# Six more weight blocks of a two-layer model as seven block products, with two of the four weight sums on GpSimd

## The chip, the cores and the metric

The kernel runs on one core of a Trainium2 chip. The metric is the time of one execution on the device in microseconds (us), the median of several runs. The engines are TensorE (PE; its weight loads are PEld), VectorE (DVE), ScalarE (ACT), GpSimd (Pool) and SyncE (SP, which issues most transfers). Each takes its instructions in the order written, and waits on semaphores that others raise.

## The reference

Two layers on 256 tokens of width 1024, all float32. Each layer is a mixer, a layer norm, a mixture of 16 experts (two per token) and a layer norm.

```python
def _mixer_ab(x, ...):                 # layer 0
    proj = x @ w_in                    # 1024 x 6152
    ...                                # retention (4 heads) and mLSTM (4 heads, causal conv on q and k)
    return concat([y_ret, y_ml]) @ w_out

def _mixer_cd(x, ...):                 # layer 1
    proj = x @ w_in                    # 1024 x 6176
    gq, gk, gv, gr, ga, sz, sxbc, sdt = split(proj)
    log_alpha = log_sigmoid(ga @ gla_w_alpha + gla_b_alpha) / 16
    y_gla = head_norm(gla(gq, gk, gv, log_alpha)) * silu(gr)      # 4 heads
    xs, bm, cm = split(silu(causal_conv(sxbc)))
    y = ssd(xs * dt, dt * a, bm, cm) + d * xs                     # 4 groups of 4 heads
    y_ssd = head_norm(y * silu(sz))
    return concat([y_gla, y_ssd]) @ w_out
```

## The kernel before, in words

**Units.** The input weights of a mixer are cut into twelve units of 1024 rows by 512 columns (2 MB), ab0 to ab11 and cd0 to cd11, each in a slot of a ring of six. Both halves of a slot are loaded by SP as soon as the unit six places ahead has been used up. In layer 1, cd0 and cd1 are the queries and keys of the linear attention (GLA), cd2 and cd3 its values, cd4 and cd5 its gate, cd6 to cd9 the inputs of the causal convolution, cd10 and cd11 the gate z of the state-space part (SSD). A *token unit* leaves tokens on the partitions (16 matmuls of 512 columns), a *feature unit* leaves features there (32 of 256 columns). Every float32 matmul shows as two records in the trace.

**A unit as seven products.** ab2 to ab11 are computed otherwise (`first_product`, `other_products`, line 833 for the token form and 836 for the feature form). Tokens and weights are cut into 2 by 2 blocks, and seven products of 4 matmuls of 256 columns (or 8 of 128) give what eight blocks would. Some factors are sums of blocks: two token sums at first and two more (`mix_tokens`), and four weight sums per unit. In the order in which TensorE makes them, the products are:

1. first: bank 0 or 3, plain blocks; ScalarE copies it (`first_copy`)
2. second: bank 1, plain blocks; VectorE adds it (`blend` 0)
3. third: onto the first, with weight sum `sums[0]`; ScalarE copies (`sum_copy` 0)
4. fourth: bank 2 afresh, with weight sum `sums[1]`
5. fifth: onto the third, with the weight block that was changed in place; ScalarE copies (`sum_copy` 1), VectorE adds bank 2 (`blend` 1)
6. sixth: onto the fifth; ScalarE copies (`sum_copy` 2)
7. seventh: onto bank 2, with the block that is changed in place last; VectorE adds (`blend` 2)

The first product of the next unit is made between the fifth and the sixth, in `gap`; `fill` is work of another kind between the second and the third. The semaphore `product_done` counts the second, third, fifth, sixth and seventh product, `combined` the blends, `copied` the later copies. A unit's fourth product waits until all blends of the unit before are done, and its seventh until its own second blend is.

All four weight sums are made by VectorE (`mix_weights`: three; `mix_last`: the fourth, after the second product). They are 128 partitions by 1024 elements each.

**The second mixer's side work.** Each engine's order is written out by hand. VectorE: copies of cd0 and cd1, the gates' running sums (`alpha`, four scans into `bcum`), then per head `gla_head` (scaled queries and eight blocks of scaled keys, whose exponentials ScalarE makes), `p_gla` (masked scores), `y_gla` (norm and gate; it waits for a root from ScalarE). TensorE makes `s_gla` (scores) once `gla_head` is done and `y_gla` (values) once `p_gla` is. Then `taps` (the conv's three later taps per tile on VectorE, the first and the SiLU on ScalarE), `ssd_args`, `ssd_probs`, `ssd_gate`, `ssd_norm` per group, between `s_ssd` and `y_ssd` on TensorE. GpSimd only issues some transfers: among them the store of the SSD running sums and their reload, spread over all partitions, in two halves.

## Time and profile before

| | |
|---|---|
| median of 3 runs | 972.47 us (971.17 to 973.62) |
| the profiled execution | 973.6 us, span 971.8 us |
| TensorE busy | 939.7 us, 97% |
| VectorE busy | 358.6 us, 37% |
| ScalarE busy | 233.4 us, 24% |
| GpSimd busy | 15.3 us, 2% |
| HBM read | 277.04 MB |

The span is from the first instruction to the last in the trace; the execution's own time is measured around it. Busy time of TensorE is from the start of matmuls to their modelled ends, so two neighbouring groups overlap a little: the time from start to start is the better price. The first mixer runs to about 250 us, its experts to 476, the second mixer from there to about 737, its experts to the end.

### The profile page before, as it was taken

What the parts mean: (1) busy time and instruction counts of PE and PEld (TensorE: products, weight loads), DVE (VectorE), ACT (ScalarE), POOL (GpSimd) and SP (SyncE); (2) the same over time, 40 slices, a digit from 0 to 9 for tenths busy, and PEclk for the clock granted to TensorE, in tenths of its full rate; (3) what the DMA queues carried; (4) which work ended last, traced back from release to release, by engine and by line L of the source; (5) the groups of instructions that cost most, each with busy time, mean ns of one, the idle gap of its engine ahead of it and who ended that gap; (6) DMA issues with size and microseconds to landing.
All of it is one profiled execution on the core that took longest, in us unless ns stands there. A gap on an engine that the chain in (4) does not pass through costs nothing.

```text
span 971.8 us, 10789 instructions
## 1 busy us (share of the span) xinstructions
PE 939.7 (97%) x4272; PEld 550.7 (57%) x4272; DVE 358.6 (37%) x847; ACT 233.4 (24%) x497; POOL 15.3 (2%) x29
## 2 busy tenths in 40 slices
PE   8999999999999999999999999999999999999996
PEld 7888988844533454332584568887545334443332
DVE  4656687423522111120335334654225121131204
ACT  1123352420311121110303343432522121111101
POOL 2000000000000000000000000000000000000001
PEclk9999999999999999999999999999999999999999
DMA  8974434462999999999995234434646999999994
GB/s 273 341 263 170 154 111 169 146 244 98 349 379 421 422 416 423 398 419 417 392 326 213 87 104 156 173 131 170 221 173 259 351 421 421 420 422 419 419 419 169
DMA packets 66934, 278.87 MB, mean 287 GB/s; under 512 B 8980, under 2 KB 9344, under 8 KB 44096
## 3 DMA queue, kind: packets, MB, share of 16 engines
q1 hardware_dynamic: 65008, 271.60, 71.9%
q0 software_dynamic: 1872, 6.53, 1.7%
q8 instruction: 37, 0.61, 0.3%
q14 instruction: 17, 0.14, 0.0%
HBM read 277.04 MB, written 1.06 MB: 286 GB/s over the span
## 4 chain that ended last, share of the span: by engine, by line
PE 83%; DMA 10%; DVE 3%; issue 1%; ACT 1%; SPq 0%; DVEq 0%
PE bank L766 67%; PE bank L833 10%; DMA ring<-in_moe_w_up 7%; DMA ring<-in_moe_w_down 2%; PE bank L1212 2%; PE bank L836 2%; DMA ring<-in_w_in_ab 1%; PE bank L1217 1%; PE bank L1607 1%; PE bank L925 1%; DVE feat L2333 1%; ACT feat L1675 0%; PE bank L1119 0%; PE bank L1160 0%; DVE stat L2642 0%
## 5 line engine op out<-in xcount | busy, mean ns | idle before, releaser
L766 PE MATMUL bank<-ring,feat 128*64 128x512 f32 (+1 forms) x1152 | 228.7, 595 | 3.0 <-ACT feat L1675 2.7
L766 PE MATMUL bank<-ring,hT 128*64 128x512 f32 (+1 forms) x544 | 159.3, 595 | 7.2 <-DMA ring<-in_moe_w_up 3.6
L766 PEld LDWEIGHTS bank<-ring,feat 128*64 128x64 f32 (+1 forms) x1152 | 74.2, 131 | 142.6 <-issue 131.0
L1675 ACT ACTIVATE feat<-bank 32x512 f32<-32x512 f32 (+3 forms) x128 | 60.9, 494 | 382.1 <-PE bank L766 241.4
L766 PE MATMUL bank<-hT,ring 128*128 128x256 f32 x640 | 140.2, 380 | 0.8 <-DMA ring<-in_w_in_ab 0.8
L766 PEld LDWEIGHTS bank<-hT,ring 128*128 128x128 f32 x640 | 121.7, 191 | 17.2 <-DMA ring<-in_w_in_ab 1.5
L766 PE MATMUL bank<-ring,yT 128*128 128x512 f32 x256 | 112.8, 595 | 0.0
L766 PEld LDWEIGHTS bank<-ring,hT 128*64 128x64 f32 (+1 forms) x544 | 60.3, 149 | 89.5 <-issue 83.2
L2632 DVE COPY feat<-bank 32x512 f32<-32x512 f32 (+1 forms) x56 | 38.5, 687 | 145.9 <-PE bank L766 145.4
L766 PEld LDWEIGHTS bank<-ring,yT 128*128 128x128 f32 x256 | 47.9, 190 | 55.3 <-issue 55.1
L2622 DVE TENSOR_TENSOR feat<-feat,bank 128x512 f32<-128x512 f32 x16 | 11.0, 688 | 169.5 <-PE bank L766 169.5
L1675 ACT ACTIVATE tok<-bank 128x256 f32<-128x256 f32 (+1 forms) x52 | 22.4, 432 | 135.3 <-PE bank L833 72.8
L833 PE MATMUL bank<-ring,hT 128*128 128x256 f32 x192 | 44.6, 380 | 0.0
L833 PEld LDWEIGHTS bank<-ring,hT 128*128 128x128 f32 x192 | 36.2, 190 | 5.6 <-issue 0.8
L766 PEld LDWEIGHTS bank<-tok,h 128*128 128x128 f32 x128 | 32.5, 331 | 11.4 <-issue 11.1
L766 PE MATMUL bank<-tok,h 128*128 128x256 f32 x128 | 37.7, 430 | 0.9 <-DVE tok L2509 0.9
L2344 DVE SCALAR_TENSOR_TENSOR feat<-bank,cols_cd,feat 128x255 f32<-128x255 f32 (+2 forms) x48 | 23.1, 482 | 25.7 <-ACT feat L1675 24.6
L1675 ACT ACT_TABLE_LOAD x25 | 32.1, 1283 | 2.2 <-PE bank L766 1.7
L1212 PE MATMUL bank<-feat 128*128 128x512 f32 x64 | 30.9, 607 | 1.0 <-ACT feat L1675 1.0
L833 PE MATMUL bank<-ring,yT 128*128 128x256 f32 x128 | 30.2, 379 | 0.0
L833 PEld LDWEIGHTS bank<-ring,yT 128*128 128x128 f32 x128 | 24.1, 190 | 3.1
L2148 DVE TENSOR_TENSOR tok<-tok,bank 128x256 f32<-128x256 f32 x30 | 12.5, 418 | 29.3 <-ACT tok L1675 23.2
(276 smaller groups left out, 803.8 us busy)
## 6 DMA issues: line engine op xcount, KB each, us to landing
ring<-in_moe_w_up SPq DMA_DIRECT2D x60, 1024.0 KB, 16.1
ring<-in_moe_w_down SPq DMA_DIRECT2D x56, 1024.0 KB, 11.6
ring<-in_moe_w_gate SPq DMA_DIRECT2D x48, 1024.0 KB, 14.3
ring<-in_w_in_ab SPq DMA_DIRECT2D x24, 1024.0 KB, 9.0
ring<-in_w_in_cd SPq DMA_DIRECT2D x24, 1024.0 KB, 13.4
ring<-in_w_out_ab SPq DMA_DIRECT2D x8, 1024.0 KB, 6.1
ring<-in_moe_w_gate SPq DMA_DIRECT2D x16, 512.0 KB, 5.1
ring<-in_moe_w_down SPq DMA_DIRECT2D x16, 512.0 KB, 17.6
```

Of the source, the lines that this page charges most:

```text
L766: return nc.tensor.matmul(o, l, r, start=start, stop=stop)
L833: last = nc.tensor.matmul(o, x[:, k, :], y[:, k, :], start=first and k == 0, stop=k == 3, skip_group_check=True)
L836: last = nc.tensor.matmul(o[:, cols], y[:, k, cols], x[:, k, :], start=first and m == 0 and k == 0, stop=k == 3, skip_group_check=True)
L925: last = nc.tensor.transpose(bank[b][:, k * SEQ + t * P:k * SEQ + (t + 1) * P], src[:, t, c * P:(c + 1) * P], ident)
L1212: return nc.tensor.matmul(bank[4 + 2 * t + q][:, :], selw_t[:, t, :], ye[:, t, q * 512:(q + 1) * 512], start=start, stop=False, skip_group ...
L1217: last = nc.tensor.transpose(bank[0][:, c * P:(c + 1) * P], hid[:, c:FF:FF // P], ident)
L1607: last = nc.tensor.matmul(bank[b][e * SSD_HD:(e + 1) * SSD_HD, c * SEQ + j * P:(c + 1) * SEQ], xdt[:, j, hd * SSD_HD:(hd + 1) * SSD_HD], p ...
L1675: return nc.scalar.activation(o, i, f, **kw)
L2148: V.tensor_tensor(o, o, held_part(name, 1 if i == 0 else 2), ALU.add).then_inc(combined, 1)
L2344: ins = V.scalar_tensor_tensor(out=o, in0=bank[b][:, (m % 2) * SEQ:(m % 2 + 1) * SEQ - back], scalar=cols[:, c:c + 1], in1=o, op0=ALU.mult ...
L2622: V.tensor_tensor(hid, sil, bank[3][:, :], ALU.mult) \
L2632: ins = V.tensor_copy(ye[r, t, 512:1024], bank[3][r, :])
```

## The change

Units cd2 to cd5 (token form) and cd10 and cd11 (feature form) are computed as seven products, too. Their token sums are four more instructions of VectorE, their blends three per unit. In both mixers VectorE makes two weight sums per unit, `sums[1]` and `sums[0]` (now from `sums[1]` and a plain block), and GpSimd the other two, in place: an early one behind the first weight sum, needed by the fifth product, and a last one behind the second product, needed by the seventh. VectorE's first sum for the next unit waits for GpSimd's last. ScalarE's copies are more and smaller, and cut `gla_head` in halves. GpSimd's sums stand in its queue among the transfers of the running sums. TensorE's order in the second mixer is new: the GLA scores and values are in `fill` and `gap`, those of the last head around and behind the halves of cd6. Not shown below are the bank plan, the waits on claimed banks (eased to what each bank needs), and the moved addresses of z and of one set of SSD decays.

```diff
+        token_mix = (token_mix, [by_chunk(conv_raw[:, r:r + 2, :], P) for r in (0, 2, 4, 6)])
...
+            def mix_weights(name):
+
+                unit, w, sums = fast[name], unit_weights(name), mixes(name)
+                pool.wait_ge(weights_mixed, 2 * unit + 1)
+                nc.gpsimd.tensor_tensor(w[:, 0:4, SEQ:], w[:, 0:4, SEQ:], w[:, 0:4, 0:SEQ], ALU.subtract) \
+                    .then_inc(pool_mixed, 1)
+                pool.wait_ge(weights_mixed, 2 * unit + 2)
+                pool.wait_ge(product_done, 5 * unit + 1)
+                nc.gpsimd.tensor_tensor(w[:, 4:8, 0:SEQ], w[:, 4:8, 0:SEQ], sums[0], ALU.subtract).then_inc(pool_mixed, 1)
+
+            for n in range(2, 12):
+                mix_weights(f"ab{n}")
             lns = [("ln_mix_g", "ln_mix_b", 0), ("ln_ffn_g", "ln_ffn_b", 0),
                    ("ln_mix_g", "ln_mix_b", 1), ("ln_ffn_g", "ln_ffn_b", 1)]
             for n, (g, b, l) in enumerate(lns):
@@ -731,16 +753,21 @@
                 elif n == 0:
                     pool.wait_ge(y_done, 8)
                 else:
+                    mix_weights("cd2")
                     pool.wait_ge(gate_ok, 2)
                     pool.dma_start(cum_out, gate_row[0:SSD_HEADS, 3, :]).then_inc(cum_stored, 16)
+                    for unit in ("cd3", "cd4", "cd5"):
+                        mix_weights(unit)
                     pool.wait_ge(cum_stored, 16)
-                    pool.wait_ge(h_ready, 2 * TB)
+                    pool.wait_ge(product_done, 5 * fast["cd5"] + 5)
                     for half in range(2):
                         if half:
+                            mix_weights("cd10")
                             pool.wait_ge(cum_used, 1)
                         rows = cum_out[half * KC:(half + 1) * KC, :].rearrange("(o h) t -> o (h t)", o=1)
                         pool.dma_start(cum_rows.rearrange("p r n -> p (r n)"), rows.to_broadcast([P, KC * SEQ])) \
                             .then_inc(cum_in, 16)
+                    mix_weights("cd11")
                     pool.wait_ge(cum_used, 2)
...
-                pe.wait_ge(weights_mixed, 4 * unit + 3)
-                pe.wait_ge(tokens_mixed, 3)
+                pe.wait_ge(weights_mixed, 2 * unit + 2)
+                pe.wait_ge(tokens_mixed, 4 * (name[:2] == "cd") + 3)
                 pe.wait_ge(first_copied, unit + 1)
-                product(name, 0, token_mix[1], sums[0], False).then_inc(product_done, 1)
+                product(name, 0, token_sums(name)[1], sums[0], False).then_inc(product_done, 1)
                 if plan[name][2]:
                     pe.wait_ge(stored[2], plan[name][2])
                 if unit:
                     pe.wait_ge(combined, 3 * unit)
-                product(name, 2, token_mix[2], sums[1], True)
+                product(name, 2, token_sums(name)[2], sums[1], True)
                 pe.wait_ge(copied, 3 * unit + 1)
-                product(name, 0, token_mix[0], weight_block(n, 0, 1), False).then_inc(product_done, 1)
+                pe.wait_ge(pool_mixed, 2 * unit + 1)
+                product(name, 0, token_sums(name)[0], weight_block(n, 0, 1), False).then_inc(product_done, 1)
                 if gap:
                     gap()
                 pe.wait_ge(copied, 3 * unit + 2)
-                pe.wait_ge(tokens_mixed, 4)
-                product(name, 0, token_mix[3], weight_block(n, 1, 1), False).then_inc(product_done, 1)
-                pe.wait_ge(weights_mixed, 4 * unit + 4)
+                pe.wait_ge(tokens_mixed, 4 * (name[:2] == "cd") + 4)
+                product(name, 0, token_sums(name)[3], weight_block(n, 1, 1), False).then_inc(product_done, 1)
+                pe.wait_ge(pool_mixed, 2 * unit + 2)
                 pe.wait_ge(combined, 3 * unit + 2)
                 product(name, 2, token_block(1, 1), weight_block(n, 1, 0), False).then_inc(product_done, 1)
...
-            token_unit("cd2", unit_no(1, 2), (0,), range(0, 2))
+            first_product("cd2", unit_no(1, 2))
             fold_groups("alpha_in", "cd_sum", GLA_RANK)
...
+            def alphas():
+                wait_stored(pe, "alpha_in", 5)
...
+            def step_turns():
+                first_product("cd3", unit_no(1, 3))
...
+            other_products("cd2", unit_no(1, 2), alphas, step_turns)
...
+            def second_gla_unit():
+                first_product("cd4", unit_no(1, 4))
+                s_gla(0)
+
+            def third_gla_unit():
+                first_product("cd5", unit_no(1, 5))
+                s_gla(1)
+
+            other_products("cd3", unit_no(1, 3), None, second_gla_unit)
+            other_products("cd4", unit_no(1, 4), lambda: y_gla(0), third_gla_unit)
+            other_products("cd5", unit_no(1, 5), lambda: y_gla(1), lambda: s_gla(2))
+            feature_unit("cd6", unit_no(1, 6), plain, (0,))
+            s_gla(3)
             y_gla(2)
-            token_unit("cd5", unit_no(1, 5), (1,), range(KC // 2))
-            s_gla(3)
-            token_unit("cd5", unit_no(1, 5), (1,), range(KC // 2, KC))
+            feature_unit("cd6", unit_no(1, 6), plain, (1,))
             y_gla(3)
-            feature_unit("cd6", unit_no(1, 6), plain)
             feature_unit("cd7", unit_no(1, 7), plain)
...
+            first_product("cd10", unit_no(1, 10))
+
+            def first_ssd_scores():
+                first_product("cd11", unit_no(1, 11))
+                s_ssd(0)
+                s_ssd(1)
+
+            def last_ssd_scores():
+                y_ssd(1)
+                s_ssd(2)
+                s_ssd(3)
+
+            other_products("cd10", unit_no(1, 10), None, first_ssd_scores)
+            other_products("cd11", unit_no(1, 11), lambda: y_ssd(0), last_ssd_scores)
...
+            first_copy("cd2")
...
+            sum_copy("cd2", 0)
...
-                if hd:
+
+            def gla_blocks(hd, half):
+                if hd and half == 0:
                     wait_ready(act, f"s_gla{hd - 1}", first_of(f"s_gla{hd - 1}"))
-                for i in range(SEQ // GLA_BLOCK):
+                for i in range(4 * half, 4 * half + 4):
                     s, k = i // 4 * P, 8 * hd + i
                     fn(k_blocks[:, i, :], bcum[:, hd, s:s + P], ACT.Exp, scale=-1.0 / GLA_TAU,
                        bias=gate_col[:, 0, :, :].rearrange("p a b -> p (a b)")[:, k:k + 1]).then_inc(kexp, 1)
 
+            sum_copy("cd2", 1)
+            first_copy("cd3")
             act.wait_ge(gate_a, 5)
             gla_head(0)
-            token_unit("cd2", ACT.Copy)
-            token_unit("cd3", ACT.Copy, (0,))
+            sum_copy("cd2", 2)
+            gla_blocks(0, 0)
+            sum_copy("cd3", 0)
+            gla_blocks(0, 1)
+            sum_copy("cd3", 1)
+            first_copy("cd4")
+            sum_copy("cd3", 2)
             gla_head(1)
-            token_unit("cd3", ACT.Copy, (1,))
+            gla_blocks(1, 0)
+            sum_copy("cd4", 0)
+            gla_blocks(1, 1)
+            sum_copy("cd4", 1)
+            first_copy("cd5")
+            sum_copy("cd4", 2)
             gla_head(2)
-            token_unit("cd4", ACT.Silu)
+            gla_blocks(2, 0)
+            sum_copy("cd5", 0)
+            gla_blocks(2, 1)
+            sum_copy("cd5", 1)
+            activate("cd4", ACT.Silu)
+            sum_copy("cd5", 2)
             root(1, mv[:, :, 1])
             root(1, mv[:, :, 1])
             gla_head(3)
-            token_unit("cd5", ACT.Silu)
+            gla_blocks(3, 0)
+            gla_blocks(3, 1)
+            activate("cd5", ACT.Silu)
             root(1, mv[:, :, 1])
             root(1, mv[:, :, 1])
...
-            conv_unit("cd9", 20, cols_cd, ROWS_CD["conv_w"] + 48, ROWS_CD["conv_b"], 12, 20)
+            conv_unit("cd9", 20, cols_cd, ROWS_CD["conv_w"] + 48, ROWS_CD["conv_b"], 12, 20, (0, 1))
+            first_copy("cd10")
+            conv_unit("cd9", 20, cols_cd, ROWS_CD["conv_w"] + 48, ROWS_CD["conv_b"], 12, 20, (2,))
+            sum_copy("cd10", 0)
+            conv_unit("cd9", 20, cols_cd, ROWS_CD["conv_w"] + 48, ROWS_CD["conv_b"], 12, 20, (3,))
+            sum_copy("cd10", 1)
+            first_copy("cd11")
+            sum_copy("cd10", 2)
             ssd_exps(1)
+            sum_copy("cd11", 0, 1)
             z_unit("cd10", 0)
+            sum_copy("cd11", 2)
             z_unit("cd11", 4)
...
-                V.tensor_tensor(w[:, 0:4, SEQ:], w[:, 0:4, SEQ:], w[:, 0:4, 0:SEQ], ALU.subtract) \
-                    .then_inc(weights_mixed, 1)
-                dve.wait_ge(weights_mixed, 4 * unit + 2)
-                V.tensor_tensor(sums[0], w[:, 4:8, SEQ:], w[:, 0:4, SEQ:], ALU.subtract).then_inc(weights_mixed, 1)
-
-            def mix_last(name):
-
-                unit, w, sums = fast[name], unit_weights(name), mixes(name)
-                dve.wait_ge(product_done, 5 * unit + 1)
-                dve.wait_ge(weights_mixed, 4 * unit + 3)
-                V.tensor_tensor(w[:, 4:8, 0:SEQ], w[:, 4:8, 0:SEQ], sums[0], ALU.subtract).then_inc(weights_mixed, 1)
+                dve.wait_ge(weights_mixed, 2 * unit + 1)
+                V.tensor_tensor(sums[0], sums[1], w[:, 0:4, 0:SEQ], ALU.add).then_inc(weights_mixed, 1)
...
+            mix_tokens(1, 0, 2, 1, 3)
...
+                    mix_weights("cd2")
...
+            blend("cd2", 0)
...
             for hd in range(HEADS):
                 link(V.tensor_tensor_scan(bcum[:, hd, :], dec[:, 0, 0:SEQ], gtmp[:, hd, :], 0.0, ALU.mult, ALU.add))
 
+            blend("cd2", 1)
+            mix_weights("cd3")
...
             gla_head(0)
+            blend("cd2", 2)
+            blend("cd3", 0)
+            blend("cd3", 1)
+            mix_weights("cd4")
             p_gla(0)
             gla_head(1)
+            blend("cd3", 2)
+            blend("cd4", 0)
+            blend("cd4", 1)
+            mix_weights("cd5")
             p_gla(1)
+            blend("cd4", 2)
             gla_head(2)
+            blend("cd5", 0)
+            blend("cd5", 1)
             y_gla(0)
+            p_gla(2)
             y_gla(1)
-            p_gla(2)
+            blend("cd5", 2)
             gla_head(3)
             p_gla(3)
...
             taps("cd8", 16, cols_cd, cw, 16, 8, 16)
             xs_by_dt()
+            mix_weights("cd10")
             ssd_args(1)
-            taps("cd9", 20, cols_cd, cw, 16, 12, 20)
+            taps("cd9", 20, cols_cd, cw, 16, 12, 20, (0, 1, 2))
+            blend("cd10", 0)
+            taps("cd9", 20, cols_cd, cw, 16, 12, 20, (3,))
+            blend("cd10", 1)
+            mix_weights("cd11")
             ssd_probs(0)
+            blend("cd10", 2)
             ssd_probs(1)
+            blend("cd11", 0)
+            blend("cd11", 1)
+            blend("cd11", 2)
             ssd_gate(0)
             ssd_args(2)
```

## Rows read from the trace of the kernel before

**Rows 1.** The page, part 1: busy time, share, instructions by engine.
```profile
PE 939.7 (97%) x4272; PEld 550.7 (57%) x4272; DVE 358.6 (37%) x847; ACT 233.4 (24%) x497; POOL 15.3 (2%) x29
```

**Rows 2.** Windows, second mixer: busy (count) by engine, clock, DMA share, GB/s.
```profile
509.00:722.00 213.00, 213.00 (x857) 142.69 (x850) 92.29 (x242) 81.73 (x159) 2.63 (x5) 1.00 0.45 163
```

**Rows 3.** Windows, the routing behind the second mixer.
```profile
720.00:740.00 20.00, 18.82 (x72) 9.59 (x71) 10.66 (x29) 2.54 (x10) 0.00 (x0) 1.00 0.22 62
```

**Rows 4.** Timeline, TensorE, first mixer: start us, us taken, [idle before].
```profile
58.62 5.41 PE L833 MATMUL bank<-tok,yT 128*128 128x256 f32 x16
...
113.88 3.74 PE L836 MATMUL bank<-hT,ring 128*128 128x128 f32 x32
...
129.80 2.02 PE L836 MATMUL bank<-hT,ring 128*128 128x128 f32 x16 [0.72 <-DVE tok L2148]
...
133.39 3.62 PE L833 MATMUL bank<-feat,yT 128*128 128x256 f32 x16
...
145.47 3.62 PE L833 MATMUL bank<-feat,yT 128*128 128x256 f32 x16
```

**Rows 5.** Timeline of TensorE, second mixer.
```profile
508.25 1.07 PE L766 MATMUL bank<-hT,tail_cd 128*32 128x256 f32 x16
...
581.34 27.79 PE L766 MATMUL bank<-hT,ring 128*128 128x256 f32 x128
...
673.63 7.03 PE L766 MATMUL bank<-ring,yT 128*128 128x512 f32 x16
```

**Rows 6.** Groups, VectorE, first mixer: xcount, busy us, mean ns, idle.
```profile
L2148 DVE TENSOR_TENSOR tok<-tok,bank 128x256 f32<-128x256 f32 x30 | 12.5, 418 | 29.3 <-ACT tok L1675 23.2 <-PE bank L833 5.8
L2126 DVE TENSOR_TENSOR ring<-ring 128x1024 f32<-128x1024 f32 x10 | 12.2, 1217 | 0.0
```

**Rows 7.** Timeline of all engines, end of the kernel.
```profile
964.86 1.26 POOL L750 TENSOR_TENSOR h<-h,tok 128x512 f32<-128x512 f32 x1 [124.47 <-ACT h L1675]
...
965.44 1.22 DVE L2889 SCALAR_TENSOR_TENSOR h<-h,rstd,tok 128x512 f32<-128x512 f32 x1
...
967.91 1.40 DVE L2889 SCALAR_TENSOR_TENSOR h<-h,rstd,tok 128x512 f32<-128x512 f32 x2
```

**Rows 8.** Timeline of VectorE, second mixer.
```profile
522.93 2.87 DVE L2724 TENSOR_TENSOR_SCAN yT<-yT 128x256 f32<-128x256 f32 x4
...
563.67 0.88 DVE L2780 SCALAR_TENSOR_TENSOR tok<-bank,rstd,tok 128x256 f32<-128x256 f32 x2 [12.66 <-ACT rstd L1675]
...
566.77 0.88 DVE L2780 SCALAR_TENSOR_TENSOR tok<-bank,rstd,tok 128x256 f32<-128x256 f32 x2 [0.60 <-ACT rstd L1675]
...
570.18 1.96 DVE L2753 SCALAR_TENSOR_TENSOR yT<-yT,feat 128x128 f32<-128x128 f32 x8
...
591.50 1.52 DVE L2344 SCALAR_TENSOR_TENSOR feat<-bank,cols_cd,feat 128x255 f32<-128x255 f32 x3 [0.94 <-ACT feat L1675]
...
613.65 1.65 DVE L2377 TENSOR_SCALAR yT<-bank,cols_cd 128x256 f32<-128x256 f32 x4
615.22 2.72 DVE L2817 SCALAR_TENSOR_TENSOR feat<-tok,route,consts 128x256 f32<-128x256 f32 x8
619.20 1.52 DVE L2344 SCALAR_TENSOR_TENSOR feat<-bank,cols_cd,feat 128x255 f32<-128x255 f32 x3 [1.27 <-ACT feat L1675]
...
629.21 2.48 DVE L2810 TENSOR_TENSOR tok<-bank,gate_col 128x512 f32<-128x512 f32 x4
```

**Rows 9.** Timeline of ScalarE, second mixer.
```profile
527.94 2.43 ACT L1675 ACTIVATE yT<-yT,gate_col 128x128 f32<-128x128 f32 x8
...
561.81 1.28 ACT L1734 ACT_TABLE_LOAD   x1
```

**Rows 10.** Timeline of VectorE, the gate of group 0.
```profile
656.87 0.87 DVE L2842 SCALAR_TENSOR_TENSOR feat<-feat,ssd_dc,bank 128x256 f32<-128x256 f32 x2 [5.21 <-PE bank L1607]
657.78 0.76 DVE L2851 TENSOR_TENSOR feat<-feat,tok 128x256 f32<-128x256 f32 x2
```

**Rows 11.** Windows, the stretch behind the gate transposes of the first mixer.
```profile
60.00:61.00 1.00, 1.00 (x4) 0.81 (x3) 0.00 (x0) 0.00 (x0) 0.00 (x0) 0.50 1.06 391
```

More of the change, by code:

```diff
@@ L432, in build @@
         for n in range(2, 6):
-            pair_job(f"cd{n}")
+            fast_job(f"cd{n}")
         for hd in range(2):
             job(f"s_gla{hd}", 4 + hd % 2)
-        pair_job("cd6")
         for hd in range(2):
             job(f"y_gla{hd}", 6 + hd % 2)
-        pair_job("cd7")
         for hd in range(2, 4):
             job(f"s_gla{hd}", 4 + hd % 2)
-        pair_job("cd8")
         for hd in range(2, 4):
             job(f"y_gla{hd}", 6 + hd % 2)
+        for n in range(6, 10):
+            pair_job(f"cd{n}")
         job("yturn1_0", 4, 5)
@@ L448, in build @@
             job(f"xs_turn{n}", 4 + n)
-        for n in range(9, 12):
-            pair_job(f"cd{n}")
+        for n in range(10, 12):
+            fast_job(f"cd{n}")
         job("mix1", 0, 1, 2, 3)
@@ L1524, in _ @@
-            last.then_inc(ready[b0], 1)
-            token_unit("cd2", unit_no(1, 2), (1,))
+            def alphas():
+                wait_stored(pe, "alpha_in", 5)
+                for q, b in enumerate(plan["alpha"]):
+                    claim("alpha", b)
+                    for hd in (2 * q, 2 * q + 1):
+                        last = mm(bank[b][:, (hd % 2) * SEQ:(hd % 2 + 1) * SEQ], w_alpha[:, hd * DK:(hd + 1) * DK],
+                                  gate_row[0:16, 0, :])
+                    last.then_inc(ready[b], 1)
@@ new lines, in step_turns @@
+            def step_turns():
+                first_product("cd3", unit_no(1, 3))
+                b0 = first_of("dt_cols")
+                claim("dt_cols", b0)
+                pe.wait_ge(gate_ok, 2)
+                for q, row in enumerate((2, 3)):
+                    for t in range(TB):
+                        last = nc.tensor.transpose(bank[b0][:, (q * TB + t) * 16:(q * TB + t + 1) * 16],
+                                                   gate_row[0:16, row, t * P:(t + 1) * P],
+                                                   consts[0:16, C_ID:C_ID + 16])
+                last.then_inc(ready[b0], 1)
@@ L2004, in z_unit @@
             def z_unit(name, first):
[L2005 to L2008 removed]
+                for c in (1, 0):
+                    act.wait_ge(combined, 3 * fast[name] + (2 if c else 3))
+                    act.wait_ge(copied, 3 * fast[name] + 3)
+                    rows = flat(z_rows[:, first + 2 * c:first + 2 * c + 2, :])
+                    fn(rows, rows, ACT.Silu).then_inc(activated, 1)
             def squares(g):
@@ L2335, in raw_taps, with taps @@
                         link(ins) if back < 3 else ins.then_inc(conv_sum, 1)
-            def taps(name, first, cols, w0, n_tiles, tile0, n_done):
-                for m in range(4):
+            def taps(name, first, cols, w0, n_tiles, tile0, n_done, ms=range(4)):
+                for m in ms:
                     b = list(plan[name])[m // 2]
@@ L2672, in _ @@
             scaled_router(1)
+            for t in range(TB):
+                for b in plan[f"ffn_turn{t}"]:
+                    wait_stored(dve, f"ffn_turn{t}", b)
+            mix_tokens(1, 0, 2, 1, 3)
             def gained():
@@ L2776, in y_gla @@
                 cols = slice(hd * DV, (hd + 1) * DV)
-                for bb in plan["cd4" if hd < 2 else "cd5"]:
-                    wait_stored(dve, "cd4" if hd < 2 else "cd5", bb)
+                dve.wait_ge(activated, (5 if hd < 2 else 6) * TB)
                 for t in range(TB):
```

111 lines of the change are left out of this document (34 added, 77 removed).

## The prediction

> **What bounds the kernel now.** I read the head of the page first: TensorE is busy 97% of the span, VectorE 37%, GpSimd almost never [rows 1]. Then the windows of the second mixer from its column sums to near its end: TensorE is busy in all of 213 us, at full granted clock, while the transfers use 0.45 of the DMA engines [rows 2]. Nothing waits on weights there. So every matmul taken out is worth its time, and every wait put in costs its whole length, because there is no idle time to swallow it. Behind the mixer, from 720 to 740, the DMA engines run at 0.22: the prefetch is finished and stands at full slots, which free when TensorE gets there [rows 3]. A mixer that ends later or sooner therefore moves the expert stage by as much. Last I read the queues of VectorE and ScalarE in the second mixer against TensorE's, since they serve in order.
>
> **What is saved.** In the first mixer a seven-product unit with nothing beside it starts at 133.39 and the next at 145.47: 12.08 us, or 1.73 a product; in the form for feature units two products take 3.74 less one tail of 0.17, 1.79 each, 12.5 a unit [rows 4]. A plain unit takes 27.79 less a tail, over 2, 13.8 [rows 5]. Four units save 1.77 and two save 1.35: 9.8 us.
>
> In the first mixer VectorE makes two sums of 1.22 us per unit in place of four [rows 6]. TensorE waits for that chain only once, 0.72 us before 129.80 [rows 4]: -0.6. Pool's own sums are in time there. Between the second product and the seventh lie at least four products, 6.9 us, and 512 elements took Pool 1.26 us [rows 7], so 1024 take about 2.4. The next unit's first sum now waits for Pool's last: again in time by 3 us or more. Pool's queue held only DMA issues up to here; the store of the running sums and their two reloads now stand behind Pool's sums, but the values are read by VectorE tens of us later: nothing. The token sums (four of 0.7 us, after the last transposes) and cd2's two weight sums lie in VectorE's idle time under cd0 and cd1: nothing. SP's triggers stay; a ring slot is freed by the seventh product, 2 us later than before, against a queue with slack of over half [rows 2]: nothing.
>
> **What is added: waits in the second mixer.** The seventh product of a unit adds onto bank 2, which the second blend must have read; the fourth product of the next unit starts bank 2 afresh, so it waits for the third blend of the unit before. These blends stand in VectorE's queue between parts of the gate and the linear attention.
>
> 1. Seventh product of cd2. TensorE from 509.25 (column sums start at 508.25 [rows 5] and take 1.0): first product, fold 0.9, second product, alphas 1.9, third, fourth, fifth, cd3's first, step turns 0.4, sixth: ready at 524.5. The second blend stands behind the four scans, which end at 525.8 [rows 8], and takes 0.42 [rows 6]: at least 1.7 us late. Pool's last sum for cd2 (513.7 to 516.1) meets the gate operations of VectorE; if these wait for it, as in [rows 7], the scans end 1.3 later. Taken: 2.8 (1.7 to 2.8).
>
> 2. Fourth product of cd3. VectorE after the scans: blend 0.4, cd3's two sums 2.44, small copies 0.7, then all of head 0, and only then cd2's third blend. And head 0 can't end early: its last four factors on ScalarE are queued behind the copy of cd3's third product. From the end of that product: copy 0.4, four of the eight exponentials of 2.43 us [rows 9] 1.2, the last product on VectorE 0.3, blend 0.4 and releases of 0.1: 2.4 us is the floor, whatever else happens. By the whole queue it is 3.4; with Pool's two sums in front of head 0's operations, 5.2. Taken: 5.2 (2.4 to 5.2).
>
> 3. Fourth product of cd4: the same figure, head 1 and the copy of cd4's third product. VectorE has caught up by then, so the floor: 2.4. (cd5 escapes: cd4's third blend stands ahead of head 2.)
>
> 4. Scores of head 3, in the middle of cd6. ScalarE copies cd5's sixth product and only then loads a table (1.28), takes the root (0.5) [rows 9]; from there VectorE needs what it needed from 563.67 to the end of head 3's factors at 572.1 [rows 8], 8.5, and one blend: 11.3 us after the sixth product. TensorE has 1.7 + 6.9 of work to put there. Taken: 2.7 (1 to 3.5).
>
> 5. Third product of cd10. The values of head 3 are now behind half of cd6, so VectorE starts cd6's conv taps about 10.6 us before cd7 ends (cd7's 13.8 less 3.1 for the norm of head 3, as between the two norms at 563.67 and 566.77), and it has eight tiles at 1.52 + 0.94 [rows 8]. From the end of cd7: taps until +9.1; turns, decay arguments and start of cd8's taps, 5.5 us as from 613.65 to 619.20, until +14.6; four tiles +24.5; xs 2.5, cd10's sums 2.4, arguments 2.7 [rows 8], two tiles of cd9 4.9: +37.0, and ScalarE's copy at +37.9. TensorE is there at 13.8 (cd8) + 1.7 + 13.8 (cd9) + 3.5 = +34.7. A wait of 3.2, and 5.5 if the arguments wait for Pool's sum. Taken: 5.4 (0 to 5.5).
>
> 6. Values of group 2, behind the first 6.9 us of the output projection [rows 5]. Before, the gate of group 0 came early, at 656.87 [rows 10]. Now it is queued behind cd11's third blend, so behind the last product of cd11. From there on VectorE: blend 0.5, gate 1.6 [rows 10], arguments 2.7, gate 1.6, arguments 2.7, two products 1.0: 10.3 us. Wait 3.4. No order of events shortens this one.
>
> Sum of the waits: 21.9 with Pool in VectorE's way, 16.8 without it.
>
> **The price of Pool beside VectorE.** At the end of the kernel VectorE's L2889, 512 elements with both inputs in SBUF, took 1.22 us at 965.44 while Pool's product ran to 966.12, and 1.40 for two, 0.70 each, at 967.91 [rows 7]. It seems to stand until Pool is done. The Trainium skill (SBUF — State Buffer, Who interferes with whom) says just that of a VectorE instruction with two SBUF inputs against a GpSimd instruction that reads SBUF. This speaks against the change: by that rule the sum of waits is 21.9, without it 16.8, and the trace agrees in the one place that it shows. I take 21.9.
>
> **Sum.** -9.8 - 0.6 + 21.9 = +11.5 against the profiled execution, which took 973.6 for a span of 971.8 and lies 1.1 above the median of 972.47. I take the change onto the median, a little shaded because a wait also gives the later queues time: +11, 983.5 us.
>
> **The rivals.**
> - A, no port: VectorE and Pool don't stop each other on these strided operands. Waits 1.7 + 3.4 + 2.4 + 2.7 + 3.2 + 3.4 = 16.8, so +6.4: 978.9. For it only that the trace shows one meeting. 0.22.
> - B, the clock: waits of 5 us let TensorE's clock fall. Before, it stood at 0.50, the 1.2 GHz level, at 60 us [rows 11], right behind the gate transposes and small matmuls on four rows, and sixteen matmul records from 58.62 took 5.41 us in place of 3.62: 1.8 us lost [rows 4]. Two or three such falls behind waits 2, 5 and 6 give +15 to +17: 988. Against: behind the wait of 0.72 us the matmuls kept their length [rows 4], and longer ones the trace shows none beside a mixer unit. 0.18.
> - C, the other sign: each wait delays TensorE and so gives VectorE time; if the queues run ahead of my replay, waits 1, 4 and 5 are gone and 2, 3 and 6 stay at their floors, 2.4 + 2.4 + 3.4 = 8.2. Then -9.8 - 0.6 + 8.2 = -2.2: 970.3. It decides where the waits sum to under 10.4, so it needs both TensorE late at the scans and VectorE's taps cd6 to cd9 done at least 3 us earlier in all than 2.46 a tile gives. 0.08.
> - D, the delay is made good in the expert stage, or the waits happen to equal the saving: within 0.3%. Rows 3 speak against making it good. 0.04.
>
> **How the numbers follow.** My forecast has 0.48. A difference under about 0.3% (2.9 us) can't be told from none here. Slower: forecast, A and B, 0.88; same 0.04; faster 0.08. The range goes from below A to above B: 975 to 990.
>
> **What the profile after would show.** Right: seven products at 12.1 us per bare unit in cd2 to cd5; TensorE idle of 2 to 5 us with VectorE's blend line as releaser at the seventh product of cd2 and the fourth of cd3 and cd4; idle before head 3's scores, before the third product of cd10 (releaser ScalarE) and before the values of group 2; VectorE operations with two SBUF inputs stretched to over 2 us beside Pool; Pool about 2.4 us a sum, 3.6 where VectorE's sum came first; no wait at 129.80. Wrong: TensorE still at 100% from 509 to 722, which would mean that I misread the order of a queue; unchanged lengths on VectorE (A); clock under 1.00 there (B). If the waits are there but shorter, the replay's slack was mis-sized and not the mechanism.

## The result and the profile after

The changed kernel takes 993.01 us (median of 4 runs, 992.69 to 995.02) against 972.5: ratio 1.0216 [1.0197, 1.0234], 20.5 us slower. I had forecast slower, 983.5, with 990 as the upper end. The direction was right, and the time lies 3 us above the range.

The page after, head:

```profile
span 993.2 us, 11328 instructions
...
PE 938.9 (95%) x4464; PEld 574.1 (58%) x4464; DVE 378.9 (38%) x861; ACT 239.3 (24%) x517; POOL 107.4 (11%) x61
```

Against [rows 1] TensorE is as busy as before in a span that is 21.4 us longer. That looks as if the saved products saved nothing, but part of its busy time after is spent at half clock. The timeline of TensorE in the second mixer after (start us, us taken, [idle before <- releaser]) shows the six waits and what follows them:

```profile
529.20 3.69 PE L862 MATMUL bank<-ring,hT 128*128 128x256 f32 x16 [2.83 <-DVE tok L2207]
532.73 1.89 PE L862 MATMUL bank<-tok 128*128 128x256 f32 x8
541.23 3.70 PE L862 MATMUL bank<-tok 128*128 128x256 f32 x8 [6.61 <-DVE tok L2207]
544.76 1.89 PE L862 MATMUL bank<-ring,tok 128*128 128x256 f32 x8
...
560.98 2.94 PE L862 MATMUL bank<-tok 128*128 128x256 f32 x8 [2.38 <-DVE tok L2207]
563.71 2.64 PE L862 MATMUL bank<-ring,tok 128*128 128x256 f32 x8
...
587.05 7.07 PE L795 MATMUL bank<-hT,ring 128*128 128x256 f32 x32
596.73 0.46 PE L795 MATMUL bank<-yT 128*128 128x128 f32 x2 [2.61 <-DVE yT L2812]
...
600.82 8.04 PE L795 MATMUL bank<-hT,ring 128*128 128x256 f32 x32
...
660.80 5.44 PE L865 MATMUL bank<-tok,feat 128*128 128x128 f32 x32 [2.13 <-ACT yT L1711]
...
700.18 1.71 PE L1639 MATMUL bank<-spare,tok 128*64 128x256 f32 x16 [3.30 <-DVE spare L2903]
```

Each wait stands at the place and with the releaser that the prediction gave. Undisturbed, eight records of 256 columns take 1.89. Behind the second wait they take 3.70, the next two groups behind the third 2.94 and 2.64, and the 32 records at 600.82 take 8.04 (7.07 at 587.05, undisturbed). The windows of that kernel (busy us and count by engine, granted clock, DMA share, GB/s) say why:

```profile
541.00:545.00 4.00, 3.77 (x10) 3.08 (x11) 0.41 (x2) 0.00 (x0) 0.00 (x0) 0.53 0.00 0
562.00:567.00 5.00, 5.00 (x17) 4.13 (x16) 0.12 (x1) 0.38 (x1) 0.00 (x0) 0.68 0.02 3
600.00:603.00 3.00, 3.00 (x9) 2.40 (x8) 1.55 (x6) 0.20 (x2) 0.00 (x0) 0.54 0.00 0
661.00:666.00 5.00, 5.00 (x32) 5.00 (x33) 2.38 (x6) 1.36 (x4) 0.67 (x2) 0.68 0.76 297
700.00:704.00 4.00, 3.82 (x21) 2.12 (x22) 3.97 (x11) 2.73 (x5) 0.48 (x1) 1.00 0.77 252
```

The granted clock was near 0.50, the 1.2 GHz level, for part of the time behind four of the six waits, where [rows 2] had 1.00 throughout. It stayed at 1.00 behind the 3.30 us wait at 700. I call such a stretch at the 1.2 GHz level a fall.

**Where the time went.** From cd0's first matmul to the turn of h behind the output projection, TensorE took 244.55 us before and 263.38 after: +18.8. I call this stretch the mixer's way. Its ends, before and then after:

```profile
480.47 27.85 PE L766 MATMUL bank<-hT,ring 128*128 128x256 f32 x128
...
725.02 1.06 PE L1119 MATMUL bank<-consts,h 128*128 128x128 f32 x8
```

```profile
481.41 27.85 PE L795 MATMUL bank<-hT,ring 128*128 128x256 f32 x128
...
744.79 1.04 PE L1149 MATMUL bank<-consts,h 128*128 128x128 f32 x8
```

Three kinds of added time are read from rows. The waits are 2.83 + 6.61 + 2.38 + 2.61 + 2.13 + 3.30 = 19.9. Each also costs about 0.25 of start to start that isn't counted as idle (the tail of the last group, 0.17, is no longer covered, and the first group behind it takes 0.08 more): 1.4. The four falls, taken from start to start against the same groups undisturbed, cost 1.80, 1.75, 1.68 and 1.69: 6.9. What is left, 19.9 + 1.4 + 6.9 - 18.8 = 9.4, is what the products saved; it is a difference here, and experiments 7 and 9, whose mixers have no fall, give 9.2. The other 2.6 us of the longer span lie in the first mixer and the experts (0.9 ahead of cd0, 1.6 behind the turn), and executions of the kernel before differ by nearly as much (971.17 to 973.62).

**Falls and executions.** One fall is no mark of the kernel. That of [rows 11], at 60 us, stands behind no wait. The first mixers of the kernel after and of experiment 6 are the same code, and their traces (after, then 6) show:

```profile
58.97 5.41 PE L862 MATMUL bank<-tok,yT 128*128 128x256 f32 x16
```

```profile
58.31 3.72 PE L862 MATMUL bank<-tok,yT 128*128 128x256 f32 x16
```

The fall is in the traces of before, after and experiments 3, 4, 5, 7 and 8, and missing in 1, 2, 6 and 9. It moves a span by 1.7 us, so below the mixer's way is compared rather than the whole span. Each kernel has one trace, and what its clock did in the other executions isn't known.

**Pool beside VectorE.** GpSimd's sums, and VectorE's queue around two of them, after:

```profile
530.28 3.37 POOL L737 TENSOR_TENSOR ring<-ring 128x1024 f32<-128x1024 f32 x1 [10.52 <-DVE tok L2193]
533.62 2.33 POOL L741 TENSOR_TENSOR ring<-ring,tok 128x1024 f32<-128x1024 f32 x1
```

```profile
531.37 0.18 DVE L2787 COPY gate_col<-bank 128x32 f32<-128x32 f32 x1
531.59 0.19 DVE L2788 TENSOR_SCALAR route<-bank 128x32 f32<-128x32 f32 x1
531.69 1.99 DVE L2791 TENSOR_SCALAR edge<-yT 128x4 f32<-128x4 f32 x1
533.60 0.16 DVE L2792 TENSOR_SCALAR edge<-yT 128x4 f32<-128x4 f32 x1
533.67 2.34 DVE L2793 TENSOR_SCALAR gate_col<-yT 128x32 f32<-128x32 f32 x1
536.04 0.43 DVE L2799 TENSOR_TENSOR yT<-yT 128x256 f32<-128x256 f32 x1
```

Pool's sums took 2.33 to 2.5 us, and 3.37 to 3.39 where VectorE's second sum came first, as predicted (2.4 and 3.6). But read the third line of VectorE: an instruction of four elements with a single SBUF input stands 1.99 us, exactly until Pool's first sum is done, and L2793, with 32 elements, until its second is. The two instructions ahead of them read PSUM and ran beside Pool in 0.18 and 0.19. In experiment 1, where Pool makes no sums, the same three instructions take 0.16, 0.16 and 0.18. In the first mixer, too:

```profile
144.07 0.88 DVE L2356 SCALAR_TENSOR_TENSOR tok<-bank,mv,tok 128x256 f32<-128x256 f32 x2 [1.08 <-ACT rstd L1711]
144.99 2.89 DVE L2362 TENSOR_SCALAR tok<-tok,rstd 128x256 f32<-128x256 f32 x2
147.91 0.42 DVE L2207 TENSOR_TENSOR tok<-tok,bank 128x256 f32<-128x256 f32 x1
```

Without Pool beside them the two tensor_scalar of L2362 take 0.74. Here they last until Pool's last sum of ab10 is done (147.73), and the blend behind them, ab9's third, is late for ab10's fourth product: this wait in the timeline of TensorE, in place of the 0.72 of [rows 4], which is gone:

```profile
148.48 1.97 PE L862 MATMUL bank<-feat,yT 128*128 128x256 f32 x8 [1.52 <-DVE tok L2207]
```

### The profile page after: what moved, and what is told of

Read it like the earlier page. It is cut to its first block and busy times, and to the rows that moved or that the text cites. A ratio compares the mean times of both kernels' runs of the same rounds, so it can differ in the third digit from the quotient of the medians.

```text
span 993.2 us, 11328 instructions
## 1 busy us (share of the span) xinstructions
PE 938.9 (95%) x4464; PEld 574.1 (58%) x4464; DVE 378.9 (38%) x861; ACT 239.3 (24%) x517; POOL 107.4 (11%) x61
## 5 line engine op out<-in xcount | busy, mean ns | idle before, releaser
L795 PE MATMUL bank<-hT,ring 128*128 128x256 f32 x512 | 113.3, 382 | 1.0 <-DMA ring<-in_w_in_ab 1.0
L795 PE MATMUL bank<-ring,hT 128*64 128x512 f32 x416 | 101.9, 594 | 9.0 <-issue 5.2
L795 PEld LDWEIGHTS bank<-hT,ring 128*128 128x128 f32 x512 | 98.4, 193 | 14.4 <-DMA ring<-in_w_in_ab 1.6
L795 PEld LDWEIGHTS bank<-ring,yT 128*128 128x128 f32 x256 | 47.8, 190 | 55.3 <-issue 55.1
L737 POOL TENSOR_TENSOR ring<-ring 128x1024 f32<-128x1024 f32 x16 | 54.2, 3388 | 205.2 <-DVE tok L2193 109.4
L795 PEld LDWEIGHTS bank<-ring,hT 128*64 128x64 f32 x416 | 35.6, 137 | 64.9 <-issue 59.7
L862 PE MATMUL bank<-ring,hT 128*128 128x256 f32 x288 | 67.1, 381 | 2.8 <-DVE tok L2207 2.8
L862 PEld LDWEIGHTS bank<-ring,hT 128*128 128x128 f32 x288 | 54.2, 190 | 12.0 <-issue 4.9
L1711 ACT ACTIVATE tok<-bank 128x256 f32<-128x256 f32 x56 | 21.2, 381 | 123.1 <-PE bank L862 105.6
L2207 DVE TENSOR_TENSOR tok<-tok,bank 128x256 f32<-128x256 f32 x42 | 17.4, 419 | 57.8 <-ACT tok L1711 40.8
## 6 DMA issues: line engine op xcount, KB each, us to landing
ring<-in_moe_w_down SPq DMA_DIRECT2D x56, 1024.0 KB, 11.9
```

The source lines that it names most:

```text
L737: nc.gpsimd.tensor_tensor(w[:, 0:4, SEQ:], w[:, 0:4, SEQ:], w[:, 0:4, 0:SEQ], ALU.subtract) \
L795: return nc.tensor.matmul(o, l, r, start=start, stop=stop)
L862: last = nc.tensor.matmul(o, x[:, k, :], y[:, k, :], start=first and k == 0, stop=k == 3, skip_group_check=True)
L1711: return nc.scalar.activation(o, i, f, **kw)
L2207: V.tensor_tensor(o, o, held_part(name, 1 if i == 0 else 2), ALU.add).then_inc(combined, 1)
```

## The experiments

All are compared with the kernel before on the same chip (973.1 us in the first four and in the next four, 971.9 in the last). In the diffs `-` is the changed kernel and `+` the experiment.

**1. All four sums on VectorE, nothing else undone.** The early sum stands behind the first two, the last one behind the first blend. (A switch per mixer and one wait are left out of this diff.)

```diff
                 V.tensor_tensor(sums[0], sums[1], w[:, 0:4, 0:SEQ], ALU.add).then_inc(weights_mixed, 1)
+                V.tensor_tensor(w[:, 0:4, SEQ:], w[:, 0:4, SEQ:], w[:, 0:4, 0:SEQ], ALU.subtract).then_inc(pool_mixed, 1)
...
                     V.tensor_tensor(o, o, held_part(name, 1 if i == 0 else 2), ALU.add).then_inc(combined, 1)
+                    if i == 0:
+                        V.tensor_tensor(w[:, 4:8, 0:SEQ], w[:, 4:8, 0:SEQ], sums[0], ALU.subtract).then_inc(pool_mixed, 1)
```

> All four weight sums of every unit go back to VectorE in both mixers; order of the engines otherwise as in the changed kernel. Theory 1 (Pool's sums hold up VectorE, also in instructions of a few elements): the wait of 1.5 us at the fourth product of ab10 goes, wait 2 falls from 6.6 to about 4.0 us (3.9 us of stretched small instructions less, one sum of 1.2 more), wait 1 to about 2.2, and one fall of the clock (1.8 us) goes with them: about 986.5 us. Rival (the stretched instructions lie in idle time and VectorE's work is what counts): the two extra sums of 1.2 us per unit lengthen waits 1 and 2, 995 us or more.

988.59 us, 1.0165 [1.0151, 1.0180]: 4.4 us less than the changed kernel by the medians, 5.0 by the ratios. Its timeline, and a window behind its wait 4:

```profile
526.03 3.69 PE L866 MATMUL bank<-ring,hT 128*128 128x256 f32 x16 [1.98 <-DVE tok L2214]
535.21 3.09 PE L866 MATMUL bank<-tok 128*128 128x256 f32 x8 [3.76 <-DVE tok L2214]
554.91 1.97 PE L866 MATMUL bank<-tok 128*128 128x256 f32 x8 [2.38 <-DVE tok L2214]
```

```profile
590.00:598.00 8.00, 8.00 (x28) 6.76 (x28) 2.99 (x9) 4.03 (x6) 0.00 (x0) 0.57 0.00 0
```

Waits 1 and 2 are shorter by 0.85 and 2.85, wait 5 by 0.96 (1.17), and the one at 148 is gone, with 0.79 again before 128.29; waits 3, 4 and 6 are the same to 0.01. The waits came as expected (3.76 for 4.0, 1.98 for 2.2); that a fall would go did not. There are three falls in the mixer in place of four, but the one behind wait 4 lasts twice as long, and the mixer's way, 258.66, is shorter by 4.7, the idle time alone. The profiled span is 7.1 shorter; of that 1.7 is the fall at 60 us, which this execution doesn't have. So taking the sums from Pool, with VectorE's own 2.44 us a unit paid, gives back 4.4 to 5.4 of the 20.5 us. The order of the queues is the candidate for the rest, and the next experiments test it.

**2. Spare matmuls in the gaps.** 28 matmuls of 256 columns onto an idle bank, whose output nobody reads: 14 ahead of cd3's fourth product, 5 ahead of cd4's, 5 ahead of head 3's scores, 4 ahead of cd10's third product. The sums stay on Pool.

```diff
+                warm(5, {"cd3": 14, "cd4": 5}.get(name, 0))
                 if unit:
                     pe.wait_ge(combined, 3 * unit)
```

> The changed kernel with 28 spare matmuls of 256 columns into a free bank (results unused), put ahead of four waits: 14 ahead of the fourth product of cd3, 5 ahead of that of cd4, 5 ahead of head 3's scores, 4 ahead of the third product of cd10. They fill the waits and lengthen none. Theory 1 (half clock behind each of these four waits because TensorE stood idle, 1.75 us lost each): the clock stays at 1.00 and 7 us come back, 986 us. Rival (the clock falls for another reason, such as the narrow matmuls around): 993 us, clock as before.

988.78, 1.0166 [1.0152, 1.0181]. It does more work than the changed kernel, ends its waits at the same events, and is 4.2 us faster by the medians. Behind the filled place the windows stand at full clock; behind wait 6, which isn't filled, the clock fell this time:

```profile
540.00:545.00 5.00, 5.00 (x28) 4.46 (x26) 1.67 (x3) 0.77 (x2) 0.07 (x1) 1.00 0.01 3
692.00:697.00 5.00, 5.00 (x17) 2.39 (x15) 3.43 (x9) 1.80 (x3) 0.00 (x0) 0.66 0.59 201
```

That the half clock costs time of its own is thus shown. Four falls gone and one come would be 5.2, and the mixer's way is 258.21, shorter by 5.2. The expected 7 didn't come back because of the new fall. (The profiled span is 8.2 shorter: 2.1 of that lies ahead of cd0, 1.7 of it the fall at 60 us, and 0.9 behind the turn of h.)

**3. The third blends ahead of the heads** (waits 2 and 3). On ScalarE cd2's last copy stands ahead of head 0, too.

```diff
-            gla_head(0)
             blend("cd2", 2)
+            gla_head(0)
             blend("cd3", 0)
...
-            gla_head(1)
             blend("cd3", 2)
+            gla_head(1)
             blend("cd4", 0)
```

> VectorE makes the third blend of cd2 before head 0 and that of cd3 before head 1; ScalarE makes the copy it needs before head 0. Theory 1 (waits 2 and 3 are queue order alone): both go with the half clock behind them, 6.6 + 1.8 + 2.4 + 1.8 = 12.6 us: 980.5 us. Rival (the delay only moves to the scores of heads 0 and 1, which then come late by what the blends waited for): at most half comes back, 987 us or more.

985.05 (982.34 to 987.47), 1.0133 [1.0109, 1.0156]. Waits 2 and 3 are gone, 9.0 us of idle, and none came in their place: their place in the queue was the cause. The median fell by 8.0 and the mixer's way by 11.2 (252.18), where the two waits with their tails and falls came to 13.0. The wait of 2.83, behind which the clock had held, now has a fall behind it:

```profile
529.74 5.38 PE L862 MATMUL bank<-ring,hT 128*128 128x256 f32 x16 [2.83 <-DVE tok L2207]
```

The same idle time had 3.69 behind it in the kernel after. With this one, 1.7, the mixer's way is accounted for; what the other executions had, whose times go from 982.34 to 987.47, isn't known. So a fall can't be forecast from the length of the wait alone.

**4. The tail: the gate of group 0 ahead of cd11's later blends** (wait 6), on ScalarE z of cd10 first.

```diff
             blend("cd11", 0)
-            blend("cd11", 1)
-            blend("cd11", 2)
             ssd_gate(0)
             ssd_args(2)
+            blend("cd11", 1)
             ssd_gate(1)
             ssd_args(3)
+            blend("cd11", 2)
```

> VectorE makes the gate and the next arguments of group 0 before the second blend of cd11 and those of group 1 before its third; ScalarE does cd10's SiLU before cd11's copies and cd11's after the last exponentials. Theory 1 (wait 6 is queue order): the 3.3 us before the values of group 2 go, 989.7 us. Rival (the second blend then comes late for the seventh product of cd11, or group 2's gate does for the norms): no gain, 992 us or more.

990.04, 1.0170 [1.0152, 1.0188]. Wait 6 is gone, the other five are as they were to 0.01, and none came in its place. The median is 3.0 us lower and the mixer's way 3.5 shorter (259.88): the wait of 3.30 and its tail.

**5. Pool's sums in the first mixer alone**, on the kernel before.

> The kernel before with only the first mixer changed: two of the four weight sums of ab2 to ab11 on Pool, the second mixer untouched. Theory 1 (the 0.7 us wait at ab7's seventh product goes, one of 1.5 us at ab10's fourth product comes, since conv taps on VectorE stand behind Pool): +0.8 us. Rival (as predicted, only the gain): -0.6 us. Both within 0.3%, so the trace of TensorE has to tell: idle at about 148 us or not.

973.29 (12 runs), 1.0007 [0.9997, 1.0017]. Its trace has the 1.52 us wait, at 148.28, and none at 129. My "-0.6" for this part was wrong in sign, but by about a microsecond, and the times can't tell that from nothing. The mixer's way in layer 1, whose code is that of before, takes 244.54 against 244.55.

**6 to 8. All orders together, with the sums on Pool (6), on VectorE (7), and on VectorE in the first mixer and Pool in the second (8).** Beside the edits of 3 and 4: cd2's second blend ahead of the scans, the root of head 0 ahead of cd5's last copy, cd10's first copy one tile sooner.

```diff
+            blend("cd2", 1)
             for hd in range(HEADS):
                 link(V.tensor_tensor_scan(bcum[:, hd, :], dec[:, 0, 0:SEQ], gtmp[:, hd, :], 0.0, ALU.mult, ALU.add))
...
-            blend("cd2", 1)
             mix_weights("cd3")
```

> The changed kernel, Pool's sums kept, with all six waits attacked by order: the third blends of cd2 and cd3 ahead of heads 0 and 1, cd2's second blend ahead of the scans, the root of head 0 ahead of cd5's last copy, cd10's first copy after one tile of cd9 in place of two, and the tail as in the run before. Theory 1 (queue order cost the waits, and idle time the clock): -9.8 for the products, about +0.9 in the first mixer, under 2 us of waits left, no fall of the clock in the second mixer: 966 us, faster than the kernel before. Rival (VectorE and ScalarE are short of time as such, so waits come back elsewhere): 973 us or more.

> The same orders with all four weight sums on VectorE in both mixers. Theory 1 (Pool's sums hold VectorE up more than they relieve it): no wait in the first mixer beyond the 0.7 us of before, 1 to 2 us better than with Pool: 964 us. Rival (with the waits gone Pool's relief counts): slower than with Pool by 1 us or more.

> All orders as two runs before, sums of the first mixer on VectorE, those of the second on Pool. Theory 1: better than Pool in both mixers by the 1.5 us wait at ab10, level with all sums on VectorE within 1 us: 964.5 us. Rival (the first mixer is better with Pool, as predicted): no better than Pool in both.

(6) 978.62, 1.0063 [1.0048, 1.0079]. (7) 971.10, 0.9979 [0.9967, 0.9991]. (8) 977.29, 1.0042 [1.0026, 1.0057]. All three expectations were too low, by 7 to 13 us. The rival named for (6) had the number right, and waits did come back, but its reason, that VectorE is short of time as such, isn't borne out: (7) gives VectorE more work and is faster. From (6) to (7) it is 7.5 us, and 6.2 of it, from (8) to (7), is the step in the second mixer alone. TensorE's timeline in (6), then in (7):

```profile
529.62 1.99 PE L862 MATMUL bank<-tok 128*128 128x256 f32 x8 [1.52 <-DVE tok L2195]
534.72 3.02 PE L862 MATMUL bank<-tok 128*128 128x256 f32 x8 [3.11 <-DVE tok L2207]
```

```profile
530.08 1.99 PE L866 MATMUL bank<-tok 128*128 128x256 f32 x8 [0.83 <-DVE tok L2199]
532.33 1.97 PE L866 MATMUL bank<-tok 128*128 128x256 f32 x8 [0.26 <-DVE tok L2214]
535.04 1.99 PE L866 MATMUL bank<-ring,tok 128*128 128x256 f32 x8 [0.75 <-ACT tok L1715]
```

With Pool cd2's third blend is late by 3.11, behind the small tensor_scalar that stand until Pool is done (in (6), L2791 takes 1.99 and L2793 2.33, as above), and a fall follows. A second fall stands behind its wait of 1.36 ahead of head 3's scores, where (7) has 1.34 and no fall:

```profile
588.00:589.00 1.00, 1.00 (x4) 0.77 (x3) 0.00 (x0) 0.00 (x0) 0.00 (x0) 0.50 0.00 0
```

With VectorE cd2's third blend is late by 0.26, and the window of the whole mixer shows full clock. The mixer's way is 247.81 in (6) and 240.91 in (7): 6.9, of which 3.3 is idle time and the two falls are the rest. So an extra 2.44 us of VectorE's own work per unit cost TensorE less than Pool's hold, and about half of the difference is the clock.

(7) has 4.05 us of waits left in the second mixer, of which 1.34 is ahead of head 3's scores. Its way is 3.6 shorter than before. With six waits at 0.25 beyond their idle time the products saved 3.6 + 4.05 + 1.5 = 9.2, the same as above.

**9. Two more orders on (7).** cd3's first two sums go into the 2.21 us in which VectorE waits for ScalarE ahead of the scans, and head 3's factors ahead of the norm of head 1 (diff against (7)).

```diff
+            mix_weights("cd3", early=False)
             dve.wait_ge(gate_b, 3)
...
-            mix_weights("cd3")
...
             blend("cd2", 2)
+            mix_early("cd3")
...
             p_gla(2)
-            y_gla(1)
             blend("cd5", 2)
             gla_head(3)
+            y_gla(1)
             p_gla(3)
```

> All orders changed and all four sums on VectorE, as in the earlier run of 971.1 us, and two more changes of order. (a) The first two sums of cd3 stand ahead of the scans, in the 2.21 us in which VectorE waits for ScalarE, and the early sum behind cd2's third blend. (b) The factors of head 3 stand ahead of the norm of head 1, on both engines. Theory 1 (a wait costs its idle time and about 0.25 us more of start to start, and nothing else is lost): the waits of 0.83, 0.26, 0.75 at 530 to 535 and of 1.34 at 581.5 go, 3.2 + 4 x 0.25 = 4.2 us: 967, ratio about 0.995, and TensorE takes 61.7 us from cd2's first product to cd6's first matmul. Rival: the queue of VectorE is full there (the scans come up to 1.5 us later, and the seventh product of cd2 and the third of cd10 wait in their place): 970 to 971, no gain.

967.38 (965.85 to 969.00), 0.9958 [0.9945, 0.9972]: faster than both kernels, 4.5 us under the one before by the medians and 4.1 by the ratio. Its timeline:

```profile
523.82 3.69 PE L866 MATMUL bank<-ring,hT 128*128 128x256 f32 x16 [0.82 <-DVE tok L2220]
527.35 3.62 PE L866 MATMUL bank<-tok 128*128 128x256 f32 x16
531.59 1.99 PE L866 MATMUL bank<-ring,tok 128*128 128x256 f32 x8 [0.62 <-ACT tok L1715]
...
569.66 7.07 PE L799 MATMUL bank<-hT,ring 128*128 128x256 f32 x32
576.57 0.38 PE L799 MATMUL bank<-yT 128*128 128x128 f32 x2
```

Head 3's scores don't wait any more. Of the waits at 530 to 535 two are gone, one is left at 0.62, and the scans, now later, make the seventh product of cd2 late by 0.82. Both accounts hold in part. The mixer's way, 238.66, is 5.9 us shorter than before, so 2.2 shorter than in (7) and not 4.2. From cd2's first product to cd6 it takes 62.8 with 1.4 of waits in it, 61.4 without, for which I had said 61.7. That figure had left the tails out: with two of 0.25 it is 60.9 here, and for (7), whose 63.5 holds three waits of 1.84 in all, it is 60.9 too.

## Why the prediction was right and where it failed

| term | predicted | measured |
|---|---|---|
| six units as seven products | -9.8 | -9.2 to -9.4 |
| wait 1, seventh product of cd2 | 2.8 | 2.83 |
| wait 2, fourth product of cd3 | 5.2 | 6.61 |
| wait 3, fourth product of cd4 | 2.4 | 2.38 |
| wait 4, scores of head 3 | 2.7 | 2.61 |
| wait 5, third product of cd10 | 5.4 | 2.13 |
| wait 6, values of group 2 | 3.4 | 3.30 |
| tails around the waits | 0 | 1.4 |
| falls of the clock | 0 | 6.9 |
| second mixer, sum | +12.1 | +18.8 |

**Right.** The direction, and the method: a replay of VectorE's and ScalarE's queues against TensorE's found all six places, and four of the six lengths to 0.1 us. TensorE came to cd10's third product 34.7 to 34.9 us after the end of cd7, as replayed, though the terms written there add up to 32.8: the turns between cd7 and cd8, 1.7, are missing from the list. The other sign (rival C) was far off.

**Luck.** The 2.8 of wait 1 is right by two errors that nearly cancel. Pool did meet the gate there, but L2761 took 2.27 us, and against the start of cd2 the scans ended 1.9 later than before and not 1.3; and TensorE was ready 0.9 later than the 524.5 of the replay. And the second mixer without the falls came out at 18.8 - 6.9 = +11.9, for which I had +12.1, because wait 5 was 3.3 too long and wait 2 and the tails together 2.8 too short.

**Slips in the sum.** By the figures in the prediction a token unit saves 13.81 - 12.08 = 1.73 and a feature unit 1.31, so the products give 9.5 and not 9.8, which is nearer to the 9.2 to 9.4 measured. The terms of wait 6 add up to 10.1 and not 10.3, so 3.2; measured, 3.30.

**The step that failed: the clock.** I set its price at nothing and left it to rival B, "two or three such falls", at 0.18. The one row that I had against it was a wait of 0.72 us behind which matmuls kept their length. That says nothing of waits of 2 to 6 us, and my own sum had six of those. The only fall that the trace before showed [rows 11] cost 1.8 us, and the four after cost 1.7 to 1.8 each: the price was in my hands, the count wasn't asked for. With four falls the forecast would have been 990.4, and the measured 993.01 without them is 986.1, inside the range: this term alone puts the time outside it. How many falls there would be, the trace before couldn't say; the choice of none was the error.

**Wait 2.** The term "small copies 0.7" took 4.65 us (531.37 to 536.02): I let Pool hold only instructions with two SBUF inputs. The Trainium skill (SBUF — State Buffer, Who interferes with whom) also names tensor_scalar, in modes that use both ports, as one that can contend. The trace agrees that it does, with 1.99 us for four elements; in which mode it ran, no run shows. Where I had put the meetings, at head 0's operations, there were none, because Pool was done by 535.95. With them in the sum in place of those, 3.4 + 3.95 = 7.3, against 6.61 measured.

**Wait 5.** The arguments did stretch beside Pool, from 2.72 to 4.82, as taken. VectorE started on cd6's taps when I had said, 10.5 us before cd7 ended (613.31, against 623.81), and a tile took 2.46 us from start to start, as in [rows 8]. But I had charged the gap of 0.94 once for each tile, and the last tile of a series has none behind it: the eight tiles of cd6 and cd7, the four of cd8 and the two of cd9 each ended about 0.94 sooner. VectorE came to xs 22.45 us after the end of cd7 (646.26), where I had 24.5, and the copy ended at 36.8, where I had 40.1 with Pool in the way. The gaps are 2.8 of these 3.3.

**Tails.** I priced each wait at its idle time. From start to start it is 0.25 more.

**First mixer.** "Pool's own sums are in time there" was right and beside the point: what was late is VectorE's blend behind two tensor_scalar that stood for Pool. Experiment 5 puts the whole part at about zero.

**Pool or the orders?** Of the 20.5 us, 4.4 to 5.4 go with the sums on VectorE under the changed orders (experiment 1). With the orders fixed, the same step is worth 7.5. Neither alone gives a faster kernel than before; both together do, by 2.0, and with two orders more by 4.1 to 4.5 (experiment 9), less than half of the 9.2 that the products save. Four waits of 0.3 to 0.8 us with their tails take 3.3 of that; 5.9 arrive in the mixer of the profiled execution, and 4.1 in the ratio of the times, with an interval of 2.7 to 5.3. What stays open is why one idle time has a fall behind it and the same one in another kernel none, and how often each fall comes in other executions of the same kernel.

## What to carry to other kernels

When TensorE is the bound and never waits, price a wait at its idle time, a quarter of a microsecond for the tail, and the loss of half clock behind it as this kernel's own trace shows it (here 1.7 to 1.8 us); where the sum has several waits, take a fall behind most of them as the forecast and not as a rival (here four of six, of 2.1 to 6.6 us), and don't read a difference of one fall between two traces as the work of the change. Before work goes to GpSimd "for free", list every VectorE instruction that will run beside it and reads only SBUF, the tiny ones too, and ask what stands behind them in the queue. When the replay says which blend is late, the cheap repair is its place in the queue: put what frees a bank ahead of the long side work, and put new work where the engine already waits.

## What the hardware showed that I had not expected

- A tensor_scalar of VectorE from SBUF to SBUF over 4 elements per partition stood 1.99 us beside Pool's tensor_tensor, where it takes 0.16 alone. Instructions with one input in PSUM (a copy, a tensor_scalar, blends, a scalar_tensor_tensor) ran beside Pool at their usual length.
- TensorE's granted clock fell to its 1.2 GHz level behind idle times of 2.13, 2.38, 2.61 and 6.61 us, and in the same execution not behind 2.83 and 3.30. In other kernels of this case it fell behind these two (experiments 3 and 2), held behind 2.38 (experiment 1), and fell behind 1.36 (experiment 6). In identical code without a wait, at 60 us, it fell in some executions and not in others.
- Most falls cost 1.7 to 1.8 us of TensorE's time; the one behind wait 4 of experiment 1 lasted twice as long. At the wait of 6.61 us the clock had fallen before the wait was over (0.69 from 536 to 541).
- Spare matmuls with no reader, put ahead of a wait, made the kernel 4.2 us faster.
